# High and low weight products in pairs: the order of TensorE's work inside a half tile

## What is computed

```
h @ w_in                       # projections
jnp.square(jax.nn.relu(h @ w1)) @ w2
memn @ w_kv ;  h @ w_q ;  o @ w_o ;  merged @ w_out
jnp.einsum('td,tkd->tk', x_, u)        # peer experts
```

## Time and profile before

| what | value |
|---|---|
| median of 3 runs | 4307.28 us (4301.3 to 4308.13) |
| profiled execution: own time, span | 4307.64 us, 4305.8 us |
| TensorE products busy | 4189.0 us, 97% |
| weight loads of TensorE busy | 3576.1 us, 83% |
| GpSimd busy | 3460.3 us, 80% |
| VectorE, ScalarE busy | 2309.8 us (54%), 1729.5 us (40%) |
| DMA | 814.64 MB, mean 189 GB/s |
| mean granted clock of TensorE | 0.989 |

### The profile page before, as it was taken

How to read it: one execution, slowest core, us unless ns; L and a number is a source line. 1 busy time by engine, 2 the same in 40 slices (tenths; PEclk the granted TensorE clock), 3 DMA queues, 4 the chain that set the end, 5 groups by cost and what they waited for, 6 DMA issues and landing times.

```text
span 4305.8 us, 64018 instructions
## 1 busy us (share of the span) xinstructions
PE 4189.0 (97%) x23874; PEld 3576.1 (83%) x23874; DVE 2309.8 (54%) x3342; ACT 1729.5 (40%) x2001; POOL 3460.3 (80%) x2636
## 2 busy tenths in 40 slices
PE   8999998989999999999999999999999999999998
PEld 6778786678888888888888888899888888888887
DVE  4353466633333336544323432888857847875785
ACT  4333432344444445343344434543333333433433
POOL 5754765178898888888889967988988998898898
PEclk9999999999999999999999999999999999999999
DMA  9834786045555554445455544544554554455454
GB/s 391 331 112 174 290 318 243 24 181 178 185 185 185 185 185 168 165 156 184 158 204 187 205 148 155 177 160 169 190 186 170 180 201 173 166 195 186 174 178 166
DMA packets 117477, 814.64 MB, mean 189 GB/s; under 512 B 13495, under 2 KB 18968, under 8 KB 20120
## 3 DMA queue, kind: packets, MB, share of 16 engines
q1 hardware_dynamic: 109008, 789.39, 50.4%
q10 hardware_dynamic: 8264, 22.26, 1.4%
HBM read 805.32 MB, written 6.29 MB: 188 GB/s over the span
## 4 chain that ended last, share of the span: by engine, by line
PE 59%; POOL 24%; issue 8%; DVE 6%; DMA 1%; ACT 1%; POOLq 0%; ACTq 0%; SPq 0%; DVEq 0%
POOL w_lo L474 22%; PE psum L560 18%; PE psum L564 9%; PE psum L1420 5%; PE psum L1427 5%; PE psum L1421 5%; PE psum L712 3%; PE psum L549 2%; PE psum L550 2%; PE psum L551 2%; POOL ada_acc L511 1%; DMA ring<-mixed 1%; PE psum L1350 1%; PE psum L695 1%; PE psum L697 1%
## 5 line engine op out<-in xcount | busy, mean ns | idle before, releaser
L474 POOL TENSOR_TENSOR w_lo<-ring,w_hi 128x512 fp32r<-128x512 f32 x2412 | 3131.8, 1327 | 579.3 <-ACT w_hi L1449 553.8
L1449 ACT ACTIVATE w_hi<-ring 128x1024 fp32r<-128x1024 f32 x1228 | 1291.4, 1060 | 1816.2 <-PE psum L564 1213.0
L560 PE MATMUL psum<-hc_hl,w_hi 128*128 128x512 f32 x5120 | 1310.7, 398 | 27.1 <-DVE hc_hl L2134 10.0
L560 PEld LDWEIGHTS psum<-hc_hl,w_hi 128*128 128x128 f32 x5120 | 924.5, 189 | 207.0 <-issue 16.9
L564 PEld LDWEIGHTS psum<-hc_hl,w_lo 128*128 128x128 f32 x5120 | 700.5, 191 | 52.6 <-POOL w_lo L474 1.5
L564 PE MATMUL psum<-hc_hl,w_lo 128*128 128x256 f32 x5120 | 715.8, 283 | 1.1 <-POOL w_lo L474 1.1
L1420 PE MATMUL psum<-w_hi,out_hl 128*128 128x512 f32 x1024 | 398.5, 389 | 1.3 <-DVE x_tok L3259 1.3
L1421 PE MATMUL psum<-w_hi,out_hl 128*128 128x512 f32 x1024 | 398.4, 389 | 0.0
L511 POOL TENSOR_TENSOR ada_acc<-ada_acc,ada_row 128x512 f32<-128x512 f32 x168 | 217.5, 1325 | 71.4 <-ACT ada_row L1610 67.1
L1427 PE MATMUL psum<-w_lo,out_hl 128*128 128x512 f32 x1024 | 273.7, 389 | 0.0
L560 PE MATMUL psum<-hid_hl,w_hi 128*128 128x512 f32 x1024 | 258.7, 393 | 7.6 <-DVE hid_hl L2721 7.5
(11 more groups left out here) (474 smaller groups left out, 5254.1 us busy)
## 6 DMA issues: line engine op xcount, KB each, us to landing
ring<-stream SPq DMA_DIRECT2D x620, 1024.0 KB, 4.8
ring<-mixed SPq DMA_DIRECT2D x96, 1024.0 KB, 6.9
ada_in<-ada SPq DMA_DIRECT2D x32, 1024.0 KB, 8.0
kv_dram<-kv_out ACTq DMA_DIRECT2D x32, 128.0 KB, 4.2
x<-x ACTq DMA_DIRECT2D x2, 2048.0 KB, 9.9
kv<-kv_dram ACTq DMA_DIRECT2D x2, 2048.0 KB, 9.4
mem_raw<-mem SPq DMA_DIRECT2D x2, 1024.0 KB, 6.5
ctx_raw<-ctx ACTq DMA_DIRECT2D x1, 2048.0 KB, 12.8
```

Source lines behind the costliest of these rows:

```text
L474: m = pool.tensor_tensor(w_lo[:, slot, c:c + 4], ring[:, s, h * KC // 2 + c:h * KC // 2 + c + 4], w_hi[:, slot, c:c + 4].bitcast(F32), ALU ...
L560: pe.matmul(psum[:, b, :].rearrange("p (s t) -> p s t", s=2), w_hi[:, slot, c], x_hl[c], start=start(c), stop=False, skip_group_check=True)
L1449: act.activation(w_hi[:, 2 * (s % 2) + h], ring[:, s, k], ACT.Copy).then_inc(hi_ready, 1)
```

## The change

In `half_wide` the two loops become one. The wait for `hi_ready` goes, the wait for `lo_ready` moves ahead of the first product, and the products of a block follow each other: high, low, high, low. Nothing is added or taken away elsewhere; the other engines' programs keep their order.

```
-            slot, x_hl = 2 * (s % 2) + h, {}
-            pe.wait_ge(hi_ready, g * 2 + (h + 1 - 2 * SPLIT0))
-            for c in range(KC // 2):
-                b, x_hl[c] = bank(c), hl(c)
-                pe.matmul(psum[:, b, :].rearrange("p (s t) -> p s t", s=2), w_hi[:, slot, c], x_hl[c], start=start(c),
-                          stop=False, skip_group_check=True)
+            slot = 2 * (s % 2) + h
             pe.wait_ge(lo_ready, g * 2 + (h + 1 - 2 * SPLIT0))
             for c in range(KC // 2):
-                m = pe.matmul(psum[:, bank(c), 0:T], w_lo[:, slot, c], x_hl[c][:, 0], start=False, stop=stop(c),
+                b, x_hl = bank(c), hl(c)
+                pe.matmul(psum[:, b, :].rearrange("p (s t) -> p s t", s=2), w_hi[:, slot, c], x_hl, start=start(c),
+                          stop=False, skip_group_check=True)
+                m = pe.matmul(psum[:, b, 0:T], w_lo[:, slot, c], x_hl[:, 0], start=False, stop=stop(c),
                               skip_group_check=True)
             m.then_inc(half_done, 1)
```

## The result

| | median us | lowest to highest | executions |
|---|---|---|---|
| before | 4302.47 | 4297.4 to 4312.52 | 20 |
| with the change | 4312.41 | 4303.5 to 4322.4 | 20 |

The ratio is 1.0018, with a 95% interval of 1.0011 to 1.0025: a little slower, within the 0.2% that the prediction calls no change, and 3.4 us above the upper end of its range. The forecast of 4291 us was wrong.

The account below looks back on a forecast made before the run. TensorE, its products busy 97% of the span, was taken as the bound. Terms -16.2 - 6.6 - 1.9 + 3.7 + 1.3 + 1.7 + 1.7 = -16.3 us from 4307.64 gave 4291 us; 8-in-10 range 4281 to 4309.

Parts of the forecast that it names:

- eight hidden-block waits: First down half of each MLP group: seven pairs finish before the awaited block, next half 0.84 us earlier; -6.6 us in all.
- key/value stage, without pace: Key/value stage before 260 us: uncovered low-part waits at its start, middle and last tile, +5.0 us before shorter halves give back 1.3.
- The pace: Halves outside the key/value stage: pairs at 0.3466 us make each of 816 halves 0.0199 us shorter, -16.2 us.
- Waits in the middle of a half: Low products move ahead of awaited activations: -6.6 us at MLP hidden blocks, -1.9 us at normed activations.
- normed activations: Four waits at a half's fifth block: four low products (0.48 us) come ahead of each, -1.9 us in all.
- The earlier wait: Low part awaited 1.84 us earlier: covered in steady stages, uncovered at listed places, +3.7, +1.3, +1.7 and +1.7 us.
- last MLP group's up tiles: Low part ready at 1627.97 us, TensorE there at 1626.65: +1.3 us, paid once.
- its down tiles: Last MLP group: low products start at 1658.65 us after a wait; all 16 products would then follow it, +1.7 us.
- dilated attention: Low products start at 1937.69 us after a wait; the earlier wait there costs +1.7 us.
- The high product is slower behind a low one: Rival: each high product in pairs costs 0.24 us, a half 2.87, 70 us more; about 4379 us, chance 0.06.
- The order does not change the pace: Rival: a half stays at 2.79 us, leaving +1.2 us in all; 4309 us, no change, chance 0.17.
- Waits repeat themselves: Rival: GpSimd held up by TensorE, so halves following the uncovered places wait too, adding 13.5 us; 4305 us, chance 0.09.

Follow-up runs that it names:

- again1: The changed kernel unaltered, executed once more for a second profile: 4309.24 us (span 4307.5).
- again2: The changed kernel unaltered, executed a third time for another profile: 4315.18 us (span 4313.4).
- down_norm: Kernel before, with low products ahead only of mid-half waits: seven at first MLP down halves, four at tiles awaiting normed activations; 4304.2 us against 4309.33, ratio 0.9986.
- fours: Kernel before with each half as four high, wait for the low part, four low, four high, four low: 4303.81 us, ratio 0.9989.

## Why the prediction was wrong, by its own steps

The table takes the delay against the profile of before apart, in us. "Pace" sums the changes of half lengths under 0.09 us; the rest are steps at single halves and stages without such halves.

| | first profile | again1 | again2 | forecast |
|---|---|---|---|---|
| pace, all halves | +3.0 | +5.3 | +13.5 | -17.5 |
| eight hidden-block waits | -6.7 | -6.7 | -6.7 | -6.6 |
| key/value stage, without pace | +3.2 | +3.8 | +6.5 | +5.0 |
| all else | -1.2 | -0.7 | -5.7 | +2.8 |
| span | -1.7 | +1.7 | +7.6 | -16.3 |

"All else" holds the stages from 260 to 879 us, which the change does not touch and which alone differ by -1.8 to -12.5 from before in these profiles, and the two stalls told of at the end.

**The pace** is the step that failed: "Eight of them are 2.7726 us against 2.7925 now, so a half becomes 0.0199 us shorter", for 816 halves. The 0.3466 us of the earlier trace rows was measured rightly, and many halves do have 2773 ns. What was wrong was to take one stretch of one execution as the price of the order: it has a second one, 0.3533, 6.7 ns more, and which one holds is settled stretch by stretch. In again2 258 halves are shorter than before, by 5.0 us together, and 577 longer, by 18.7 us together: the term forecast at -17.5 came out at about +13.5. The base of the sum, 4307.64 us, was high as well: 20 executions of before have a median of 4302.47.

**Waits in the middle of a half**: right, in mechanism and size, 0.84 us eight times. Of the normed activations, for which 0.48 each was forecast, the place at 2607 us gave 0.46 (its idle time fell from 1.46 to 0.99), and the idle times at 2478 us (2.33 to 1.81) and, in again1, at 1694 us (4.19 to 3.72) fell by as much; at 960 us the next half waits anew, 1.15 us at its fifth block, and the place as a whole costs 0.5.

**The earlier wait**: the places were right and the sum too high behind the key/value stage. The last MLP group's up tiles cost 1.6 in again1 (forecast 1.3); its down tiles nothing in the end (forecast 1.7), a delay of 1.9 being taken up by later waits; dilated attention 0.8 (forecast 1.7). GpSimd keeps up elsewhere, as forecast. The second half tile of the program starts at 21.63 us in the first profile (forecast 22.1; 20.17 before).

**The rivals.** "The high product is slower behind a low one" was the nearest: pairs of over 0.350 us do occur, with single distances of 0.236 to 0.241 behind a low product, as the earlier trace rows had hinted. But only a part of the halves has them, so the pace costs 3 to 14 us in these profiles and not 70. "The order does not change the pace" gave 4309 us, near the median, for another reason, and so by luck: two paces, one shorter and one longer than before, that cancel in part. "Waits repeat themselves" fell.

The Trainium skill, "TensorE: Matmul & The Clock Gate", section "Back-to-back issue gap", gives a formula by columns alone, N / 2.4 GHz + 2.5 ns, for the gap of a single product by itself; by it a half is an estimated 8 x (216 + 109) = 2600 ns in any order. For a stream in which each product has its weight load, as here, the section says that both set the distance, that the formula gives too much at 512 columns, and that about 131 ns were measured there. The runs agree with neither size: in undisturbed halves 512 columns take 224 to 241 ns and 256 columns 111 to 120, and the same 16 products take 2773 to 2832 ns, by their order. No run here parted the weight loads' share from the products'.

What stays open: what in the chip makes a repeated sequence take one length or another, and what picks between the two of the pairs. In the changed kernel the pace changes over where the row of pairs is broken, by a stall or by other products between two halves; that the break causes it was not tried by itself.

## What to carry to other kernels

A pace read from one stretch of one execution is one sample: look for the same pattern in other places, behind each break above all, and in a second execution, before it is multiplied by hundreds. Where products of two sizes share an engine, try several orders of the same work and look at the spread of the lengths, not the mean alone; the steady order (two and two) beat the one with the shortest possible time. A product that waits in the middle of a sequence should stand behind all that doesn't need it: that was worth 0.84 us each time with seven low products moved ahead, 0.72 with six and 0.48 with four.

## What was not expected of the hardware

By their order alone the same 16 products take 2787, 2793, 2807, 2813 or 2820 ns a half, and strict pairs have two paces for one and the same order, 346.6 and 353.3 ns a pair.

And an instruction of VectorE at times stood 9 to 20 us long beside an unbroken run of GpSimd. In the first profile of the changed kernel, VectorE in the last MLP group, GpSimd there, and TensorE behind them:

```profile
1659.56 12.94 DVE L2758 TENSOR_TENSOR t_half<-t_half 128x256 f32<-128x256 f32 x1
```

```profile
1654.74 17.48 POOL L474 TENSOR_TENSOR w_lo<-ring,w_hi 128x512 fp32r<-128x512 f32 x14
```

```profile
1669.39 0.40 PE L560 MATMUL psum<-hid_hl,w_hi 128*128 128x512 f32 x1
1669.63 0.28 PE L562 MATMUL psum<-hid_hl,w_lo 128*128 128x256 f32 x1
1673.88 0.79 PE L560 MATMUL psum<-hid_hl,w_hi 128*128 128x512 f32 x1 [3.96 <-DVE x L2777]
```

Before, the same VectorE instruction took 1.23 us:

```profile
1666.40 1.23 DVE L2760 TENSOR_TENSOR t_half<-t_half 128x256 f32<-128x256 f32 x1
```

With the change it ends at 1672.50, when GpSimd's run has ended at 1672.22. TensorE then waits for the PSUM banks that VectorE should have emptied, and its next product takes 0.79 us instead of 0.40, with the granted clock at 0.50 from 1673 to 1677: the lower of its two levels, after an idle time of 3.96 us. The halves there lose 6.6 us. In again2 the same befalls a VectorE product of 128x2048 at 1916.47 (12.19 us, 2.29 before), which ends 2.15 us after GpSimd's run, and TensorE loses 9.5 us in two halves where again1 loses 1.7.

At these two instructions no other of the 14 profiled executions shows such a stretch. Elsewhere it is common: in ten of the 14, that of before among them, one multiplication of VectorE in the last stage takes 19.6 to 19.8 us, 1.38 in the other four, and ends 0.55 us after GpSimd's run has ended. The rows of before:

```profile
4249.02 31.30 POOL L474 TENSOR_TENSOR w_lo<-ring,w_hi 128x512 fp32r<-128x512 f32 x25
```

```profile
4261.06 19.81 DVE L3316 TENSOR_TENSOR y_tok<-x_tok,gain_row 128x512 f32<-128x512 f32 x1
```

The four without it are some 1.6 us shorter behind the last half tile. down_norm has one more, at 1959.98 us (8.72, 1.39 elsewhere). All 13 end 0.3 to 2.2 us after the run of GpSimd. That GpSimd's run holds VectorE is what the rows suggest, and no run here tried it; a run alone is not enough, since in fours the same multiplications take 1.4 us beside a run of 46 us. The Trainium skill, "SBUF — State Buffer", section "SBUF: two separate sides", tells of a port pair that a VectorE instruction with two inputs in SBUF and a GpSimd instruction hold against each other, each for one whole instruction. By the rows the wait is longer than that: it goes on through ten instructions of GpSimd, 1.25 us each (17.48 / 14).
